# A streaming encoder step: inputs loaded first, pooling sums by one scan on VectorE, transposes by DMA instead of TensorE

## What is computed

```
u = rmsnorm(x);  proj = u @ w_in                     # 1024 -> 5632 columns = 44 chunks of 128
xl, gl, xp, gp, ml, mp = split(proj)                 # 8, 8, 4, 8, 8, 8 chunks
xc  = depthwise causal conv, 4 taps, of xl
r,i = sigmoid(blockdiag(xc) + b);  a = exp(-8 r softplus(-lam))
h_t = a_t h_(t-1) + sqrt(1 - a_t^2) * i_t * xc_t      # recurrence over time
A   = h * silu(gl)
pooled = (mean of the last 2/4/8/16 frames, by group of 128 channels) - xp
B   = (pooled @ w_pool + b) * scale * silu(gp)
x   = x + (sigmoid(ml) * A + sigmoid(mp) * B) @ w_out
x   = x + sigmoid(rmsnorm(x) @ w_ple_gate) * (p @ w_ple)
y   = rmsnorm(x)                                      # and the last states of conv, recurrence, pooling
```

## Time and profile before

| | |
|---|---|
| median of 3 runs | 1117.07 us (1112.11 to 1254.04) |
| the profiled execution | 1117.64 us, span of its slowest core (core 3) 1116.0 us |
| spans of the other cores | 1101.1 to 1112.5 us |
| PE / DVE / ACT / POOL busy | 1010.1 / 916.4 / 821.0 / 623.8 us |
| granted TensorE clock, mean | 0.956 of full speed (core 3) |
| moved by DMA | 171.25 MB, 153 GB/s |

### The profile page before, as it was taken

One profiled execution on the slowest core, in us unless ns is written; L12 is line 12 of the kernel. 1 busy time (PEld: TensorE's weight loads), 2 busy tenths in 40 slices (PEclk: granted clock), 3 DMA queues, 4 the chain that ended last, 5 costly groups with the idle time before them and its releaser, 6 DMA issues.

```text
span 1116.0 us, 19302 instructions; the slowest of 8 cores (1101.1 to 1116.0 us)
## 1 busy us (share of the span) xinstructions
PE 1010.1 (91%) x5185; PEld 476.3 (43%) x5185; DVE 916.4 (82%) x1260; ACT 821.0 (74%) x1316; POOL 623.8 (56%) x708
## 2 busy tenths in 40 slices
PE   2398997867999999999999899999999999999994
PEld 1143333323444455444455444454444454444441
DVE  3458988898489989999889988889999988998753
ACT  5368777756688887878788677888788777777643
POOL 2013555555346676567646666566766675666644
PEclk9589999998999999999999999999999999999997
DMA  8888776556355464455444355554354443454211
GB/s 227 224 228 215 227 188 163 160 160 218 117 163 162 130 190 139 150 166 172 132 136 149 114 156 155 149 165 144 121 158 144 129 135 117 144 147 132 86 50 75
DMA packets 115918, 171.25 MB, mean 153 GB/s; under 512 B 10521, under 2 KB 60953, under 8 KB 115813
## 3 DMA queue, kind: packets, MB, share of 16 engines
q1 hardware_dynamic: 114229, 166.88, 49.6%
q0 software_dynamic: 1440, 2.62, 1.6%
q10 hardware_dynamic: 144, 0.52, 0.1%
HBM read 143.50 MB, written 29.12 MB: 155 GB/s over the span
## 4 chain that ended last, share of the span: by engine, by line
PE 57%; DVE 15%; issue 9%; ACT 6%; SPq 6%; POOL 5%; DMA 1%; DVEq 0%; ACTq 0%; POOLq 0%
PE psum L656 35%; PE psum L1242 8%; PE psum L1182 7%; DVE wk L801 4%; SPq L606 2%; PE psum L1262 2%; DVE wk L1082 2%; DVE xrt L1285 1%; DVE wk L891 1%; SPq L434 1%; POOL xrt L1278 1%; DVE wk L867 1%; PE psum L1217 1%; DVE wk L902 1%; ACT wk L860 1%
## 5 line engine op out<-in xcount | busy, mean ns | idle before, releaser
L656 PE MATMUL psum<-ut,wr 128*128 128x512 bf16 x2816 | 671.2, 391 | 11.2 <-DVE wk L1088 7.0
L656 PEld LDWEIGHTS psum<-ut,wr 128*128 128x128 bf16 x2816 | 277.3, 100 | 346.5 <-issue 72.0
L801 DVE SCALAR_TENSOR_TENSOR wk<-xlw,cvec,wk 128x512 f32<-128x512 f32 x192 | 217.1, 1131 | 16.3 <-ACT wk L775 2.2
L666 POOL TENSOR_TENSOR stat<-stat,negh 128x1 f32<-128x1 f32 x99 | 94.0, 950 | 229.8 <-DVE stat L663 221.3
L1242 PE MATMUL psum<-wpg,u2t 128*128 128x512 bf16 x528 | 121.2, 383 | 4.6 <-ACT u2t L1229 2.9
L1182 PE MATMUL psum<-wout,mg 128*128 128x512 bf16 x512 | 119.7, 388 | 4.4 <-POOL mg L1098 4.4
L1098 POOL TENSOR_TENSOR mg<-mg,wk 128x512 bf16<-128x512 bf16 x64 | 89.6, 1400 | 35.2 <-DVE wk L1088 21.8
L1278 POOL TENSOR_TENSOR xrt<-xrt 128x1024 f32<-128x1024 f32 x30 | 81.1, 2703 | 31.2 <-DVE xrt L1270 24.2
L1082 DVE SCALAR_TENSOR_TENSOR wk<-wk 128x512 f32<-128x512 f32 x64 | 74.5, 1164 | 18.8 <-ACT wk L1069 12.2
L923 POOL TENSOR_TENSOR mg<-wk 128x512 bf16<-128x512 f32 x64 | 87.5, 1368 | 0.1
L1204 ACT ACTIVATE junk<-xrt 128x1024 bf16<-128x1024 f32 x60 | 63.9, 1066 | 29.0 <-POOL xrt L1278 28.4
(11 more groups left out here) (159 smaller groups left out, 1735.3 us busy)
## 6 DMA issues: line engine op xcount, KB each, us to landing
wr<-win_bf SPq DMA_DIRECT2D x264, 256.0 KB, 2.9
xs<-xp SPq DMA_DIRECT2D x33, 512.0 KB, 4.4
wpg<-w_in SPq DMA_DIRECT2D x30, 512.0 KB, 8.1
xrt<-xp SPq DMA_DIRECT2D x29, 512.0 KB, 4.3
yp<-xrt SPq DMA_DIRECT2D x29, 512.0 KB, 3.5
win_bf<-wr SPq DMA_DIRECT2D x44, 256.0 KB, 6.9
xrt<-w_in SPq DMA_DIRECT2D x14, 512.0 KB, 8.3
xrt<-w_ple_gate SPq DMA_DIRECT2D x8, 512.0 KB, 4.5
```

Source lines behind the costliest of these rows:

```text
L656: P.op("pe", lambda e, kc=kc: e.matmul(bank.ap[:, col:col + N], lhsT=wv[:, kc, :], rhs=ut_v[:, kc, :], start=(kc == 0), stop=(kc == 7)), r ...
L666: P.op("pool", lambda e: e.tensor_tensor(out=st.ap[:, 1:2], in0=st.ap[:, 2:3], in1=NEGH.ap, op=ALU.pow), reads=[st.buf, NEGH.buf], writes= ...
L801: P.op("dve", lambda e, j=j, k=k: e.scalar_tensor_tensor(out=acc_v, in0=xlw_v[:, :, 3 - j:3 - j + L], scalar=CV.ap[:, CW + k * 8 + c:CW + ...
```

## The change

- The input rows of T0 and T1 (eight blocks of 512 KB) are all loaded ahead of everything else on the SP queue; x blocks 5 to 7 get buffers of their own, and blocks 8 to 10 are loaded at slots 6 to 8. The first `w_in` chunks, the small vectors and the gate weights follow; the pool weights, the sample's states and the last norm's weights come later than before (`wpl`, `scl`, `sl`), and the set-up of constants is split in two. One dummy activation on ScalarE stands at the start. T1's first two blocks are transposed ahead of slot 0.
- `f_win` is one VectorE instruction: for g = 0 an addition, for g = 1 to 3 a scan s_t = s_(t-1) + x_t - x_(t-w), for which `xpw` gets 16 columns of zeros in front.
- The cast to `xcb` is an activation on ScalarE, a step of its own (`xcb`, 0.44 or 0.57 slots after xl).
- The transposes of T2 to T7 and of the sample in `a_tile` (25 blocks), and those of all 33 `c_tile`, are transposing DMAs on the SP queue; the copies on ScalarE go with them. T0 and T1 (8 blocks) keep TensorE. The factor 0.5 that the copy of p's transpose applied is replaced by carrying 2x through the last part (`scalar=2.0` in L1190's place, eps of 4e-6).
- All offsets of the table change. Those that the prediction uses: in `c_tile`, transpose at 1.2943 and `wpg` matmuls at 2.3466 slots after its start (before 1.4893 and 1.9249); the last block of a tile is transposed 1.0502 slots ahead of the tile's first use (before 0.9327).

```
-    XPW = [sb("xpw%d" % i, [128, 527], F32) for i in range(2)]
+    XPW = [sb("xpw%d" % i, [128, 16 + 527], F32) for i in range(2)]
     XLWS = sb("xlws", [128, 4 * 35], F32)
-    XPWS = sb("xpws", [128, 4 * 47], F32)
-    SA = sb("sa", [128, 527], F32)
-    SBB = sb("sbb", [128, 527], F32)
-    SAS = sb("sas", [128, 188], F32)
-    SBS = sb("sbs", [128, 188], F32)
+    XPWS = sb("xpws", [128, 4 * 63], F32)
+    SA = sb("sa", [128, 543], F32)
+    SBB = sb("sbb", [128, 543], F32)
+    SAS = sb("sas", [128, 4 * 63], F32)
...
-        return XS[i] if i < 3 else MG0ST[i - 3] if i < 5 else XS[(i - 5) % 3]
+        return XS[i] if i < 3 else MG0ST[i - 3] if i < 5 else (XR[2], TGC, WX)[i - 5] if i < 8 else XS[(i - 8) % 3]
+
+    WX = T(WKT.ap[:, 4096:5120], WORK[8].buf)
...
+    for i_ in (4, 5, 6, 7):
+        load_x(i_)
+
     P.op("pool", lambda e: e.memset(NEGH.ap, -0.5), writes=[NEGH.buf])
+    for t_, n_ in ((XPW[0], 1), (XPW[1], 1), (XPWS, 4)):
+        P.op("pool", lambda e, t_=t_, n_=n_: e.memset(t_.ap.rearrange("p (s w) -> p s w", s=n_)[:, :, 0:16], 0.0),
+             writes=[t_.buf, halo_buf(t_)])
+    P.op("act", lambda e: e.activation(out=JUNK.ap[:, 0:1], in_=NEGH.ap, func=AF.Square), reads=[NEGH.buf],
+         writes=[JUNK.buf])
...
+    s1_ap, s1_b = WKTS.ap[:, 0:1024], [w_.buf for w_ in WORKS[0:8]]
+    s2 = T(UTS.ap.bitcast(F32), UTS.buf)
...
+        dmat = S["idx"] >= 2
...
+            if dmat:
+                P.dma(lambda e: e.dma_start(out=ut_v[:, :, j * 128:(j + 1) * 128], in_=u.ap, transpose=True), lane=u.buf,
+                      reads=[u.buf], writes=[utb.buf])
+                ut_cnt[S["idx"]] = ut_cnt.get(S["idx"], 0) + 1
+                return
...
-        if i < 3 or 5 <= i < NAT - 3:
-            at(sc_ + 0.01, lambda: load_x(i + 5 if i < 3 else i + 3))
+        if i == 7:
+            at(sc_ + 0.01, lambda: wk_free["p"].extend([8, 9]))
+        elif 8 <= i < NAT - 3:
+            at(sc_ + 0.01, lambda: load_x(i + 3))
         at(t2, f_tr, d, ("_sc", ), "_tr")
-        at(t2 + 0.07, f_cp, d, ("_tr", ))
+        if not dmat:
+            at(t2 + 0.07, f_cp, d, ("_tr", ))
...
+        def f_xcb():
+            acc = d["acc"]
             claim(xcb, ("xc", S["idx"], c))
-            P.op("dve", lambda e: e.tensor_copy(out=xcb.ap[:, 0:N], in_=acc.ap[:, 0:N]), reads=[acc.buf],
+            P.op("act", lambda e: e.activation(out=xcb.ap[:, 0:N], in_=acc.ap[:, 0:N], func=AF.Copy), reads=[acc.buf],
                  writes=[xcb.buf])
...
-        at(o + F["gates"], f_gates, d, ("_conv", ), "_gates")
+        at(o + F["xcb"], f_xcb, d, ("_conv", ), "_xcb")
+        at(o + F["gates"], f_gates, d, ("_xcb", ), "_gates")
...
             need(hb, ("xp", S["idx"], g))
-            src, src_v = xpw, xpw_v
-            for i in range(g + 1):
-                sh = 2 ** i
-                lo = 2 ** (i + 1) - 1
-                dst = tmp[i % 2]
-                dst_v = dst.ap[:, 0:nseg * W].rearrange("p (s w) -> p s w", s=nseg)
-                claim(dst, ("w", S["idx"], g))
-                P.op("pool", lambda e, dst_v=dst_v, src_v=src_v, lo=lo, sh=sh: e.tensor_tensor(
-                    out=dst_v[:, :, lo:W], in0=src_v[:, :, lo:W], in1=src_v[:, :, lo - sh:W - sh], op=ALU.add),
-                    reads=[src.buf, hb], writes=[dst.buf])
-                src, src_v = dst, dst_v
+            src = tmp[par]
+            n0 = nseg * (16 + W)
+            src_v = src.ap[:, 0:n0].rearrange("p (s w) -> p s w", s=nseg)[:, :, 16:16 + W]
+            claim(src, ("w", S["idx"], g))
+            if g == 0:
+                P.op("dve", lambda e: e.tensor_tensor(out=src_v[:, :, 1:W], in0=xpw_v[:, :, 1:W],
+                                                      in1=xpw_v[:, :, 0:W - 1], op=ALU.add),
+                     reads=[xpw.buf, hb], writes=[src.buf])
+            else:
+                P.op("dve", lambda e: e.tensor_tensor_scan(
+                    out=src.ap[:, 16:n0], data0=xpw.ap[:, 16:n0], data1=xpw.ap[:, 16 - wnd:n0 - wnd],
+                    initial=0.0, op0=ALU.add, op1=ALU.subtract), reads=[xpw.buf, hb], writes=[src.buf])
...
-                    out=xr.ap[:, hf * 512:(hf + 1) * 512], in0=dd[hf].ap, scalar=0.5,
-                    in1=xr.ap[:, hf * 512:(hf + 1) * 512], op0=ALU.mult, op1=ALU.add), reads=[xr.buf, dd[hf].buf],
+                    out=xr.ap[:, hf * 512:(hf + 1) * 512], in0=xr.ap[:, hf * 512:(hf + 1) * 512],
+                    scalar=2.0, in1=dd[hf].ap, op0=ALU.mult, op1=ALU.add), reads=[xr.buf, dd[hf].buf],
...
-            tb, tb2 = newbank(), newbank()
-            d["t"] = (tb, tb2)
-            tbv, tb2v = tb.ap.bitcast(BF16), tb2.ap.bitcast(BF16)
-            for c in range(8):
-                P.op("pe", lambda e, c=c: e.transpose(out=tbv[:, c * 128:(c + 1) * 128],
-                                                      in_=u2.ap[:, c * 128:(c + 1) * 128], identity=IDB.ap),
-                     reads=[u2.buf, IDB.buf], writes=[tb.buf])
-            for c in range(2):
-                P.op("pe", lambda e, c=c: e.transpose(out=tb2v[:, c * 128:(c + 1) * 128],
-                                                      in_=pb.ap[:, c * 128:(c + 1) * 128], identity=IDB.ap),
-                     reads=[pb.buf, IDB.buf], writes=[tb2.buf])
-
-        def f_tc():
-            tb, tb2 = d["t"]
             claim(u2t, ("u2t", k))
             claim(pt, ("pt", k))
-            P.op("act", lambda e: e.activation(out=u2t.ap, in_=tb.ap.bitcast(BF16), func=AF.Copy), reads=[tb.buf],
-                 writes=[u2t.buf])
-            P.op("act", lambda e: e.activation(out=pt.ap, in_=tb2.ap.bitcast(BF16)[:, 0:256], func=AF.Copy,
-                                               scale=0.5),
-                 reads=[tb2.buf], writes=[pt.buf])
-            relbank(tb, tb2)
+            P.dma(lambda e: e.dma_start(out=u2t.ap.rearrange("p (k n) -> p k n", k=8), in_=u2.ap, transpose=True),
+                  lane=u2t.buf, reads=[u2.buf], writes=[u2t.buf])
+            P.dma(lambda e: e.dma_start(out=pt.ap.rearrange("p (k n) -> p k n", k=2), in_=pb.ap, transpose=True),
+                  lane=pt.buf, reads=[pb.buf], writes=[pt.buf])
...
-                a_tile(ft + j, -2.75 + 0.2 * j, -3.2 + 0.2 * j, -3.1 + 0.2 * j)
+                a_tile(ft + j, -3.37 + 0.1 * j, -3.6 + 0.1 * j, -3.42 + 0.1 * j)
         elif S["idx"] == 1:
             for j in range(4):
-                t2 = OFF[3]["a1"] + OFF[3]["a1d"] * j
-                a_tile(ft + j, t2, t2 - OFF[3]["a1q"], t2 - OFF[3]["a1s"])
+                if j < 2:
+                    a_tile(ft + j, -2.6 + 0.1 * j, -3.0 + 0.1 * j, -2.9 + 0.1 * j)
+                else:
+                    a_tile(ft + j, OFF[3]["a1"] + OFF[3]["a1d"] * (j - 2), -2.4 + 0.1 * (j - 2), -2.3 + 0.1 * (j - 2))
...
-    at(-3.5, lambda: [chunk_load() for _ in range(2)])
-    at(-3.45, vec_loads)
-    at(-3.4, lambda: load_x(4))
-    at(-2.65, lambda: [chunk_load() for _ in range(2)])
-    at(-2.6, small_loads)
-    at(-2.55, lambda: [chunk_load() for _ in range(2)])
-    at(-2.5, small_loads1)
-    at(-3.38, small_loads2)
+    at(-4.0, lambda: chunk_load())
+    at(-3.99, vec_loads)
+    at(-3.98, lambda: chunk_load())
+    at(-3.2, lambda: [chunk_load() for _ in range(2)])
+    at(-3.1, small_loads)
+    at(-3.05, lambda: [chunk_load() for _ in range(2)])
+    at(OFF[3]["wpl"], small_loads1)
+    at(OFF[3]["scl"], small_loads2)
+    at(6.0, lambda: load_x(8))
+    at(7.0, lambda: load_x(9))
+    at(8.0, lambda: load_x(10))
```

73 lines of the change are left out of this document (44 added, 29 removed), and 6 rows, old and new, of the table OFF.

## The result

The changed kernel takes 1073.6 us (1072.6 to 1077.1, 4 runs); the kernel before, on the same chip, 1112.1 and 1117.1 us in the runs compared. The ratio is 0.9638, 95% interval 0.9584 to 0.9692: 3.6% faster. The profiled execution took 1074.5 us (span of core 7, 1072.9 us). Executions in which the cores of a die ran at a lower granted clock are left out of every ratio.

The account below looks back on a forecast made before the run. TensorE was taken to bound the stage from 300 to 1050 us, VectorE's order 84 to 300 us. Terms: 1117.6 - 29 - 10 - 12 + 3 = 1069.6, forecast 1069 us, range 1036 to 1130 us.

Parts of the forecast that it names:

- Transposes off TensorE, -29: Mostly the stage from 300 us: moving 25 and 33 block transposes to DMAs saves TensorE 29 us, counted in full.
- In the stage from 300 us I price all this at 0: Latency and queue waits of the transposing DMAs, and their added DMA time, were to cost nothing in the long stage.
- My cover: Transposing DMAs, taken at 5 us, hide inside a 15 us lead; `wr` loads behind them on SP have 17 us.
- rival A: From 300 us, transposes fill the DMA engines beyond 6.5 us per large one; kernel slower, 1130 us at 7.5; chance 0.17.
- Sums and cast: VectorE: +3 us net work, 25 us relief from GpSimd, about 894 us busy; ScalarE takes 64 casts at 0.6 us.
- the two keep their distance, and TensorE still sets the pace: Long stage: VectorE falls 2.4% and TensorE 2.9%, so TensorE remains the bound there.
- First pass and inputs, -10 and -12: First pass: -10 us as the cast leaves VectorE's order; start: -12 us from inputs first, between +7 and -26.
- So from about 27 us on TensorE can go at the pace of arrival: Start: up to nine chunks, 31 us of work, by 58 us against 5 done before; up to 26 us gained.
- The end, +3: Drain: a 1.02 us copy and 0.55 us of TensorE become a DMA of 3 to 17 us; +3 us.
- B: Rival: TensorE's gain goes into new waits, 0.3 us per step, +20, and the start gives nothing; 1104 us, chance 0.2.
- C: Rival: the first pass gains in full, -26 and -25 in place of -12 and -10; 1041 us, chance 0.13.
- the signs: TensorE busy near 980 us, DMA share 0.5 to 0.65, landings under 7, taps nearer 0.82, under 25 idle 84 to 270.

## Where the prediction was right, and which of its steps failed

The forecast was 1069 us and 1073.6 was measured. The median span fell by 38.7 us where the sum says 48. That it came so near is in part luck: two steps of the sum failed in opposite directions, and a third term got its size from another cause than the one named. Its terms by stage:

**Transposes off TensorE, -29.** The work was sized rightly: TensorE's work in the long part is 26.2 us less than with the transposes on TensorE in the otherwise changed kernel (the long part without its pauses), and the rest of the 29 lies in the parts beside it. But the step that failed is the sentence "In the stage from 300 us I price all this at 0". Undoing them costs 10.2 us in the long part, not 26, since they bring 15.5 us of pauses: 10.6 of these lie in the 45 us behind the first `wout` matmul (21.4 against 10.8), the rest is spread. My cover was counted from the lead of 15 us and a landing of 5; the landing is 3.7, so neither was wrong, but at the hand-over a lead in slots isn't a lead in time: the first block's steps come out of one late chain, and no other block has work under which its transpose could hide. Its `u` is ready at 270.5 us, the queue stands behind the transpose of T2's `ub` until 272.4 and issues at 272.9, and the matmuls start at 278.7. So of the wait of 6.10 us some 2 are the queue; that a wait of one DMA holds the next I had counted for the `wr` loads alone. The landing of 3.7 us (4.7 for `ut`) was nearer to the ordinary load, as chosen, and the engines' time per transpose, some 1.5 us, is far from rival A's 6.5. The Trainium skill's page "VectorE: DVE Perf Modes" ("The three transpose paths") would have eight blocks take 10.5 us by estimate, and the Trainium skill's page "DMA: Bandwidth & Descriptors" ("Latency and other measured facts") 1.0 us by estimate; the landings of 3.7 and 4.7 us stand between them, and the engines' 1.5 us near the second.

**Sums and cast.** VectorE fell to 869.9 where I had 894: the scans cost 31.5 us (31.1 predicted) and the additions 5.6 (6.6), but the relief from GpSimd was 46.5 + 2.1 = 49 us where I took 25 (60 by the run that undoes the sums alone), mostly outside the taps: these fell by 13.7 us, and the two lines that multiply beside them, L867 before and L903 after, and L1082 before and L1123 after, by 17.9 and 22.2. One line rose, L891 before and L927 after, by 12.1: with all offsets changed, which lines meet GpSimd's work changed too. I had looked for it in one line because only that one had an undisturbed row, and took a mean near 0.82 us for the sign of it; the taps' mean is 1.06. The casts on ScalarE took 0.627 us, 0.6 predicted. The sentence that "the two keep their distance, and TensorE still sets the pace" is the second step that failed: undone alone, the sums cost 16.7 us and the cast 10.7 in the long part, which I had left at zero (the cast with a limit of 34.5 if it failed). So TensorE didn't set the pace alone: with the transposes off it, each of the two VectorE parts cost 10 us or more in this stage.

These two errors, 15 us too much for the transposes and nothing for the VectorE parts, nearly cancel, which is luck: the long part fell by 28.2 us, and my terms say about 26. The single-part runs don't add up to it (10.2 + 16.7 + 10.7 = 37.6), and the transposes alone on the kernel before lose 8%, or 4.6% with their lead (2.7% on the cores whose clock stayed up). The parts depend on each other; how much of the result belongs to the other offsets that changed with them wasn't separated.

**First pass and inputs, -10 and -12.** Measured -12.4 for both, by one pair of runs (-12 to -17 with the scatter of the first part), where the terms say -22. The step that failed is "So from about 27 us on TensorE can go at the pace of arrival". The first product came at 29.61, as said, but then the chunks weren't there: SP's queue stood 8.55 us at one small load, the second chunk was issued at 19.88, and from 20 to 40 us the DMA engines moved 163 GB/s. I had reckoned arrival at 227 GB/s from bytes alone. By 84 us 128 product matmuls are done against 123 before in these two cores, about 1 us of work, and 128 against 128.5 in the medians of the cores; the 384th product starts 0.7 us earlier, 3.9 in the median of the nine kernels with this start. So the term of -12 measured -1 to -4. The -10 of the first pass had the right size and only in part the cause that I gave it: it was the wait for the cast, which fell from 9.9 to 4.3 us while a wait of 14.9 us for ScalarE (L1110) came, which I had as a risk. The product times say 9.6 us, all of it lost again with the sums on GpSimd and 3.7 of it with the cast on VectorE.

**The end, +3.** The drain and the last part together went from 68.6 to 70.3 us, +1.7, so the sum fits and the mechanism doesn't: TensorE's part is 6.8 us shorter, and the part behind it 8.5 longer, by a chain over a single buffer that I hadn't looked at. No transposing DMA is in it.

**The rivals.** A is out (share 0.61). B's mechanism, new waits for +20, is what the runs show, at 15.5; the VectorE parts made up for it. Its own working gives more than it took: 0.3 us for each of 130 steps is 39, not 20. C is out: the first pass gained 12.4 us of its 51. Of the signs, TensorE's busy time (963.2 for 980), the share (0.61) and the landings came about as said; the taps' mean (1.06 us, nearer to 1.13 than to 0.82) and the idle time from 84 to 270 us (33.1, for less than 25) didn't, and the wait for `u2t` that was to show the forecast wrong was there.

## What to carry to other kernels

When work leaves the bounding engine, price the runner-up's parts as if it were the bound: here the two edits on the second engine cost 28.5 and 16.5 us when undone alone, and the one on the first 11.2. Work given to a third engine isn't free either, where it slows the second. A transfer with enough lead in the steady state still shows at each hand-over between stages, where the work it should hide under isn't there yet; look at that one place, and keep the old path for it if it is cheap (two of 33 blocks on TensorE gave 4.8 us). When the last matmul comes earlier, follow the chain behind it: it may be bound by one buffer and one slow addition.

## What the runs showed of the hardware

- A transposing DMA of 128x1024 bf16 takes 1.2 us of SP's queue to issue and 3.3 to 3.9 us to land (`u2t`, medians of the runs; `ut` 3.9 to 6.0); one of 128x256 takes 1.2 us to issue too, though it is a quarter of the size, and 2.3 to 2.9 us to land.
- It makes small packets: those under 512 B went from 10,521 to 81,273 with the change, 67,840 of them of 256 B, which is 1024 for each large one and 256 for each small one; and the share of the DMA engines from 0.48 to 0.61 of the window from 300 to 1000 us.
- A plain addition of 128x1024 f32 took 1.22 us on VectorE and 2.35 to 3.26 on GpSimd, and GpSimd's additions slow VectorE's instructions of two tensors beside them: the product with the input gate ran at 691 ns, and at 920 with the sums on GpSimd. GpSimd was 108 us busier there, and VectorE 21.4 although it had given up 39 us of work, so by estimate the one cost the other some 60.
- A DMA that waits holds the queue: with each large transpose issued twice, SP's queue stood 144 of 700 us for the first ones to land, and the long part grew by 38.1 us at a share of the DMA engines of 0.71.
- At the hand-over the 16 matmuls after the wait of 6.10 us took 5.60 us instead of 3.62, as at the end of the kernel before.
